# One layer of a hybrid attention decoder with experts, on one core: the loads of the first attention spread over three value tiles, the merge's reads group by group, and idle products moved and taken out

## The chip, the cores and the metric

The kernel runs on 1 core of one Trainium2 chip. The metric is the device time of one execution in microseconds (us); the times given are the median of 3 runs and their lowest and highest. All arithmetic is in float32.

## The reference, cut to what matters

The input x has 1024 tokens of 1024 channels. Per layer (there is one):

```
h = rmsnorm(x) * (1 + sc1) + sh1
proj = h @ w_in            # NSA q, keys/values, gates | dilated q/k/v | merge gates
o_nsa = g0 * compressed(q, kc, vc) + g1 * selected(q, ks, vs) + g2 * window(q, kw, vw)
o_dil = softmax-denominator mix of 3 dilated attentions (4 heads each)
merged = sigmoid(m0) * (o_nsa @ w_up_nsa) + sigmoid(m1) * (o_dil @ w_up_dil)
x = x + g1 * (merged @ w_o)
h = rmsnorm(x) * (1 + sc2) + sh2
x = x + g2 * experts(h)    # 32 experts, two per token, each silu(h@w1)*(h@w3) @ w2
out = rmsnorm(x)
```

"The first attention" is the native sparse attention (NSA): 8 heads in 4 pairs, each with a selected, a window and a compressed part. The second one is the dilated attention: 3 groups, each heads 0 to 3.

## The kernel before, in words

The program is a row of stages. At the end of a stage all engines meet, and no engine begins the next stage before the last one has arrived. The order on each engine (PE, DVE, ACT, POOL, and SP, which issues most transfers) is written out by hand, with semaphores between them. Transfers that SP issues go out in its program order.

**Condition and norm** (L242 to 485) makes h. It ends on PE with two idle products (L485). An idle product (L227) multiplies the identity by 512 columns of constants into a bank that nothing reads; it computes nothing that is used, and keeps PE at work.

**Projections** (L526 to 946). First come the rows of queries and keys, computed and stored to the DRAM tensor `d_qk`. Then come eight value tiles, v = 0 to 7. Each value tile is seven products (M1, M2, M6, M5, M7, M3, M4, in this order) that a Strassen-like scheme combines; DVE adds them up into four results (C11, C22, C12, C21). PE has four banks for them, so a product has to wait until DVE has used the product four before it (L890 to 892). For v of 4 and more every result goes into a staging slot of its own name (L603 to 607), and SP stores it to `d_v` (L645 to 649, and L622). DVE may fill the slot again in the next tile only when the store of the last one has landed (L813 to 814). At v = 4 (`HT`) SP also issues, behind the four stores of that tile, what the first attention needs (L650 to 661): 4 transfers of keys, 4 of queries (one for each pair of heads, L657) and, from `load_bias` (L969), 6 of bias. After the last tile PE has one idle product (L944).

**NSA** (L1011 to 1246) has 64 steps: for a pair of heads and a tile of 128 queries one step of selected scores, and one of window and compressed scores. In step s PE does the scores of step s, the transposes of step s - 1 and the value sums of step s - 2. It may not write the scores of step s before DVE has taken those of step s - 1 (`s_biased`, L1108 to 1110). In steps 0 and 1 there is little or nothing of the other two kinds of work.

**Dilated** (L1259 to 1468) has 6 sets in the order (i, g): sets 0 and 3 are group 0, sets 1 and 4 group 1, sets 2 and 5 group 2. SP stores each set to `d_dil`; sets 0 to 3 are waited for inside the stage (L1352), set 4 counts on `s_dil4`, and set 5 is stored by the first lines of the next stage and counts on `s_dil`. PE ends the stage with a wait for DVE's last bias and one idle product (L1408, L1409).

**Merge** (L1500 to 1835). SP issues the store of set 5, waits for sets 4 and 5 (L1546, L1547), and reads all three groups back into `dl` (L1548 to 1550). DVE, after its first additions, waits for all three (L1602), mixes the groups (`join_weights`, `join_group`) and makes `o_dil` (L1719). PE meanwhile does the products of channel tiles c = 0 and the first two of c = 1, and then turns `o_dil` (L1816), which waits for it.

**Out** (projection by w_o, router) and **experts** follow. The experts' weights are 32 x 6 MB; SP issues each 2 MB matrix when the slot that it goes to has come free, the last of them in a ring of ten slots.

Of the kernel before, what the change touches and what calls it, by code (L numbers as in the profile page):

```python
# [27 lines left out]
P = 128  # L28
# [6 lines left out]
NSA_H, NSA_KV = 8, 2  # L35
# [31 lines left out]
R_Q, R_CK, R_CV, R_SK, R_WK, R_DQ = 0, 512, 640, 768, 896, 1024  # L67
# [159 lines left out]
def idle_products(pe, k, bank, n):  # L227

    for _ in range(n):
        pe.matmul(k.psum[:, bank, :], k.ident, k.const[:, 0:BANK], start=True, stop=True)  # L230
# [11 lines left out]
def stage_condition_and_norm(k, hT, room, oT, hold, vD, ahead):  # L242

    nc = k.nc
    with ExitStack() as mem:
# [174 lines left out]
        @block.tensor  # L420
        def _(pe):
            pe.wait_ge(s_vec, 80)
            pe.wait_ge(s_const, 16)
            pe.transpose(k.psum[:, 0, 0:104], vec[:, :], k.ident[0:104, 0:104]).then_inc(s_vecps, 1)
            def turn(t):
                pe.wait_ge(s_xn, t + 1)
                for c in (2 * t, 2 * t + 1):
                    if c >= 4:
                        pe.wait_ge(s_evd if by_dve(c - 4) else s_eva, evacs[c - 4][0 if by_dve(c - 4) else 1])
                    for j in range(4):  # L430
                        d0 = (4 * (c % 2) + j) * P
                        tr = pe.transpose(k.psum[:, 4 + c % 4, j * P:(j + 1) * P], xs[:, t, d0:d0 + P], k.ident)
                    tr.then_inc(s_tr, 1)

            def bias():
                pe.wait_ge(s_oh, 32)
                pe.wait_ge(s_mask, 2)
                pe.wait_ge(s_vecT, 1)
                for i, cols in enumerate(bias_cols):
                    j, n = i % 4, cols.stop - cols.start  # L440
                    mm = pe.matmul(k.psum[G * j:G * (j + 1), B_BIAS[i // 4], 0:n], relb[:, :], onehot[:, cols],
                                   start=True, stop=True)
                    if j == 3 or i == nbias - 1:
                        mm.then_inc(s_bps, 1)

            def mod_row(i):
                if i in (1, 2):
                    pe.wait_ge(s_brow, i)
                if i == 3:
                    pe.wait_ge(s_row, 1)  # L450
                for kk in range(KD):
                    if kk == 0 or (i == 3 and kk == 4):
                        pe.wait_ge(s_ada[i + kk // 4], 16)
                    j = kk % 4
                    mm = pe.matmul(k.psum[G * j:G * (j + 1), B_ROW[i], :], condw[:, kk, :], ada(i, kk),
                                   start=(kk < 4), stop=(kk >= 4))
                mm.then_inc(s_rowps, 1)

            def mod_cols(i):
                pe.wait_ge(s_row, i + 1)  # L460
                if i == 0:
                    pe.wait_ge(s_brow, 4)
                if i == 2:
                    pe.wait_ge(s_row, 2)
                for j in range(4):
                    at = ADA_AT[i] // P + j
                    mm = pe.matmul(k.psum[:, B_COL[i // 2], at:at + 1], modrow[:, i % 2, j * P:(j + 1) * P],
                                   k.const[:, K_SEL:K_SEL + 1], start=True, stop=True)
                mm.then_inc(s_cols, 1)

            for t in range(NT):
                turn(t)
            bias()
            pe.wait_ge(s_wide, 1)
            mod_row(0)
            mod_row(1)
            mod_cols(0)
            mod_row(2)
            mod_cols(1)
            mod_row(3)  # L480
            mod_cols(2)
            mod_cols(3)
            pe.wait_ge(s_evd, evacs[-1][0])
            pe.wait_ge(s_eva, evacs[-1][1])
            idle_products(pe, k, 4, 2)  # L485


RUNS = (
# [37 lines left out]
def stage_projections(k, hT, vS, vD, gates, room, kc, vc, spare, ahead, g2row):  # L526
# [5 lines left out]
    with ExitStack() as mem:  # L532
# [55 lines left out]
        HT, HK = NT // 2, KD // 2  # L588
# [40 lines left out]
        @block.sync  # L629
        def _(sp):  # L630
            for g, (col, col2, row, scale) in enumerate(pairs):
                if g == 0:
                    continue
                if g >= 2:
                    sp.wait_ge(s_done, done(g - 2, M4))
                for s, c in enumerate((col, col2)):
                    sp.dma_start(wq[g % 2][s], w_in[:, :, c:c + P]).then_inc(s_w[g % 2], 16)
            sp.wait_ge(s_done, done(npairs - 1, M4))
            sp.wait_ge(s_used, used(npairs - 1, C21))
            for kv in range(2):  # L640
                sp.dma_start(w1c[:, kv], k.cmp_w1[0, kv].rearrange("(l p) n -> p l n", p=P)).then_inc(s_cw, 16)
                sp.dma_start(w2c[:, kv], k.cmp_w2[0, kv].rearrange("(c p) n -> p c n", p=P)).then_inc(s_cw, 16)
            for s in range(2):
                sp.wait_ge(s_store[s], 16 * npairs)
            for v in range(NV):  # L645
                for c in (C11, C22, C12, C21):
                    if set_of(v, c) > 0 and (v, c) != (NV - 1, C21):
                        sp.wait_ge(s_vused, vused(v, c))
                        store_values(sp, v, c)
                if v == HT:  # L650
                    sp.wait_ge(s_hid, 4)
                    for br, row in ((0, R_SK), (1, R_WK)):
                        for x in range(2):
                            sp.dma_start(ahead.keys[DH * x:DH * (x + 1), br, :, :],
                                         k.d_qk[row:row + P, :].rearrange("(h d) t -> d h t", d=DH)).then_inc(ahead.s_keys, 16)
                    for i in range(NSA_H // 2):
                        sp.dma_start(spare[:, i, :], k.d_qk[R_Q + P * i:R_Q + P * (i + 1), :]).then_inc(ahead.s_q[i], 16)  # L657
                    for c in (C21, C22):
                        sp.wait_ge(s_vst[SLOT[c]], 16 * stores_of(c, HT - 1))
                    sp.wait_ge(s_table, 1)  # L660
                    ahead.load_bias(sp, k, 0)
            sp.wait_ge(s_out, 3)

        @block.gpsimd
# [190 lines left out]
        def _(pe):  # L855
# [66 lines left out]
            for v in range(NV):  # L922
# [18 lines left out]
                    compressed_hidden()  # L941
                if v == HT:
                    compressed_out()
            idle_products(pe, k, 3, 1)  # L944

        return lambda sp: store_values(sp, NV - 1, C21)

# [63 lines left out]
def stage_nsa(k, vS, vD, gates, kc, vc, o_nsa, q, ahead, turned, store_last_values):  # L1011
# [5 lines left out]
    with ExitStack() as mem:  # L1017
# [27 lines left out]
        NS = len(steps)  # L1045
        OUT = 7
# [54 lines left out]
        def _(pe):  # L1101
            pe.wait_ge(s_keys, 64)
            for s in range(NS + 2):
                if s < NS:
                    i, t, kinds = steps[s]
                    if s % (2 * NT) == 0:
                        pe.wait_ge(s_q[i], 16)
                    for x in range(2):  # L1108
                        if s >= 1:
                            pe.wait_ge(s_biased, soft_no(s - 1, len(steps[s - 1][2]) - 1, x))  # L1110
                    for n, kind in enumerate(kinds):
                        lo, off = low(t, kind), offset(t, kind)
                        for col in range(0, width(t, kind), BANK):
                            for x in range(2):
                                half = slice(DH * x, DH * (x + 1))
                                w = min(BANK, width(t, kind) - col)
                                rhs = (kc[half, x, (i // 2) * NC:(i // 2 + 1) * NC] if kind == CMP else
                                       keys[half, kind - 1, i // 2, lo * P + col:lo * P + col + w])
                                at = (off + col) % BANK
                                mm = pe.matmul(k.psum[:, 2 * x + (off + col) // BANK, at:at + w],  # L1120
                                               q[half, i, t * P:(t + 1) * P], rhs, start=True, stop=True)
                                if col + BANK >= width(t, kind):
                                    mm.then_inc(s_scores, 1)
                v = s - 1
# [11 lines left out]
                v = s - 2  # L1136
                if 0 <= v < NS:
                    i, t, kinds = steps[v]
# [120 lines left out]
def stage_dilated(k, vD, spare, turned, hold, g2row, add_last):  # L1259
# [4 lines left out]
    with ExitStack() as mem:  # L1264
# [24 lines left out]
        NS = len(steps)  # L1289
# [74 lines left out]
        def _(pe):  # L1364
            for s in range(NS + 3):
# [14 lines left out]
                v = s - 2  # L1380
# [11 lines left out]
                v = s - 3  # L1392
                if 0 <= v < NS:
                    n, slot = steps[v]
                    i, g = sets[n]
# [9 lines left out]
                                               vD[:, g, slot + m + 1 - ntiles(v, m) + j, 2 * i + x, :],  # L1405
                                               start=(j == 0), stop=(j == ntiles(v, m) - 1))
                    mm.then_inc(s_summed, 1)
            pe.wait_ge(s_biased, 4 * NS)  # L1408
            idle_products(pe, k, 0, 1)  # L1409

        @block.scalar
        def _(act):
# [87 lines left out]
def stage_merge(k, hT, oT, o_nsa, room, mT, g1row, g2row, w_o, hold, s_wo, store_last_set):  # L1500
# [5 lines left out]
    with ExitStack() as mem:  # L1506
# [36 lines left out]
        @block.sync  # L1543
        def _(sp):
            store_last_set(sp)
            sp.wait_ge(k.s_dil4, 32)  # L1546
            sp.wait_ge(k.s_dil, 32)  # L1547
            for g in range(DIL_G):  # L1548
                sp.dma_start(dl[:, g].rearrange("p t h c -> p t (h c)"),
                             k.d_dil[g].rearrange("(t p) h c -> p t (h c)", p=P)).then_inc(s_dl, 16)  # L1550
            for row, c in ((g1row, 2 * D), (g2row, 5 * D)):
# [1492 lines left out]
```

## Time and profile before

| what | value |
|---|---|
| median of 3 runs | 1719.24 us (1719.05 to 1720.77) |
| the profiled execution's own time | 1718.73 us |
| its span, first to last instruction | 1716.9 us |
| PE busy | 1602.3 us (93%) |
| DVE busy | 673.9 us (39%) |
| ACT busy | 403.1 us (23%) |
| POOL busy | 176.2 us (10%) |
| mean granted TensorE clock | 0.982 of full |
| HBM read and written | 323.48 MB, 48.50 MB |

A granted clock of 1.00 is 2.4 GHz and 0.50 is 1.2 GHz. PE's busy time includes the time in which it works at the lower clock, and the idle products. In a line of a timeline the first number is the start, the second the time that the merged instructions take together, and the brackets hold the idle time of that engine just before, and who ended it. One float32 product of 128 x 128 by 512 columns shows as two MATMULs.

### The profile page before, as it was taken

Reading aid. Unit: us, or ns where it says so; the run is one execution under the profiler, and the core shown is the slowest. Engines: PE = TensorE matmul, PEld = TensorE weight load, DVE = VectorE, ACT = ScalarE, POOL = GpSimd, SP = SyncE. Lnnn points to the kernel's source line nnn. Section 1 sums busy time; section 2 is a strip of 40 time slices with the busy share of each in tenths; the row PEclk is TensorE's granted clock in tenths of the full one; section 3 lists DMA queues with packets and bytes.
Section 4 is the critical chain, followed back from the end, with each engine's and each line's share of the span. In section 5 each row is a group of like instructions: output and inputs, shape, how many; then the busy total and the mean of one; then the engine's idle time right before and its main releaser. Section 6 shows DMA issues by size and latency. Waiting matters only on the chain. (4 is left out here: it accounts for less than half of the span.)

```text
span 1716.9 us, 37104 instructions
## 1 busy us (share of the span) xinstructions
PE 1602.3 (93%) x15957; PEld 1039.2 (61%) x15957; DVE 673.9 (39%) x1682; ACT 403.1 (23%) x897; POOL 176.2 (10%) x220
## 2 busy tenths in 40 slices
PE   5999999998999999999999999999999999999873
PEld 3444445896777787644444445556777776676652
DVE  3533324312767667766654456562101001000003
ACT  4100000002666667510010002212121211211112
POOL 1205000000111010000000000001111111111100
PEclk8999999998999999999999999999999999999997
DMA  9874232235111007434352162289999999999996
GB/s 345 263 222 108 84 98 99 76 102 173 35 44 45 33 3 241 122 104 132 115 155 86 38 245 111 86 341 366 356 391 395 386 382 399 392 391 404 410 406 259
DMA packets 163745, 362.38 MB, mean 211 GB/s; under 512 B 28631, under 2 KB 111183, under 8 KB 138971
## 3 DMA queue, kind: packets, MB, share of 16 engines
q1 hardware_dynamic: 141456, 316.12, 50.1%
q0 software_dynamic: 12608, 28.01, 6.2%
q10 hardware_dynamic: 9516, 15.85, 2.6%
q8 instruction: 129, 2.11, 0.5%
q14 instruction: 36, 0.29, 0.1%
HBM read 323.48 MB, written 48.50 MB: 217 GB/s over the span
## 5 line engine op out<-in xcount | busy, mean ns | idle before, releaser
L2779 DVE TENSOR_TENSOR sb_m_hT<-psum,sb_m_sg 128x256 f32<-128x256 f32 (+2 forms) x32 | 15.3, 477 | 299.7 <-PE psum L2895 299.7
L2616 ACT ACTIVATE sb_w_o_sb<-psum,sb_rowmod 128x64 f32<-128x64 f32 (+2 forms) x256 | 81.7, 424 | 206.4 <-PE psum L2883 206.4
L862 PE MATMUL psum<-sb_vD,sb_room 128*128 128x512 f32 x240 | 104.7, 592 | 0.2 <-DVE sb_vD L743 0.2
L2895 PE MATMUL psum<-sb_w_o_sb,sb_front 128*64 128x64 f32 (+2 forms) x2560 | 91.0, 231 | 11.9 <-issue 7.3
L2895 PEld LDWEIGHTS psum<-sb_w_o_sb,sb_front 128*64 128x64 f32 x2560 | 89.0, 138 | 18.8 <-issue 18.2
L1179 ACT ACTIVATE sb_d_probs<-sb_d_probs,sb_d_nmax 128x640 f32<-128x640 f32 (+7 forms) x128 | 92.9, 735 | 12.6 <-DVE sb_d_nmax L1220 12.1
L1777 PE MATMUL psum<-sb_w_o_sb,sb_room 128*128 128x512 f32 x192 | 85.7, 603 | 0.0
L862 PEld LDWEIGHTS psum<-sb_vD,sb_room 128*128 128x128 f32 x240 | 45.5, 190 | 57.9 <-issue 57.9
L1148 PE MATMUL psum<-sb_vS,sb_room 128*64 128x65 f32 x2112 | 80.0, 226 | 0.3 <-ACT sb_room L1166 0.3
L1133 PE MATMUL psum<-sb_const,sb_d_probs 128*128 128x128 f32 x528 | 77.3, 283 | 1.6 <-ACT sb_front L1179 0.7
L1166 ACT COPY sb_room<-psum 128x512 f32<-128x512 f32 (+1 forms) x108 | 59.3, 549 | 82.6 <-PE psum L1133 82.6
L1120 PE MATMUL psum<-sb_front 64*128 64x512 f32 (+3 forms) x384 | 76.0, 500 | 2.9 <-DVE sb_d_nmax L1220 2.2
L1148 PEld LDWEIGHTS psum<-sb_vS,sb_room 128*64 128x64 f32 x2112 | 70.0, 138 | 11.3 <-issue 9.5
L753 DVE SCALAR_TENSOR_TENSOR sb_n_b_sel<-psum,sb_room 128x512 f32<-128x512 f32 x40 | 33.3, 832 | 105.5 <-PE psum L862 105.5
L1753 ACT ACTIVATE sb_room<-sb_room 128x2048 f32<-128x2048 f32 x8 | 15.3, 1910 | 246.4 <-DVE sb_room L1599 246.4
L862 PE MATMUL psum<-sb_rows,sb_room 128*128 128x512 f32 x160 | 71.1, 592 | 0.0
L1133 PEld LDWEIGHTS psum<-sb_const,sb_d_probs 128*128 128x128 f32 x528 | 58.4, 142 | 20.0 <-ACT sb_front L1179 7.3
L2627 ACT ACTIVATE sb_m_sg<-psum 128x256 f32<-128x256 f32 (+2 forms) x32 | 13.6, 425 | 238.4 <-PE psum L2895 238.4
L2895 PE MATMUL psum<-sb_w_o_sb,sb_mT 128*64 128x64 f32 (+2 forms) x1664 | 60.2, 231 | 7.7 <-issue 5.1
L2895 PEld LDWEIGHTS psum<-sb_w_o_sb,sb_mT 128*64 128x64 f32 x1664 | 58.2, 138 | 13.8 <-issue 13.8
L2895 PE MATMUL psum<-sb_w_o_sb,sb_room 128*64 128x64 f32 (+2 forms) x1536 | 59.5, 238 | 7.5 <-issue 6.0
L2895 PEld LDWEIGHTS psum<-sb_w_o_sb,sb_room 128*64 128x64 f32 x1536 | 57.9, 138 | 12.4 <-issue 12.1
(466 smaller groups left out, 2702.1 us busy)
## 6 DMA issues: line engine op xcount, KB each, us to landing
sb_front<-in_exp_w_dram SPq DMA_DIRECT2D x30, 2048.0 KB, 24.0
sb_mT<-in_exp_w_dram SPq DMA_DIRECT2D x20, 2048.0 KB, 26.6
sb_room<-in_exp_w_dram SPq DMA_DIRECT2D x18, 2048.0 KB, 23.9
sb_rows<-in_exp_w_dram SPq DMA_DIRECT2D x18, 2048.0 KB, 23.3
sb_w_o_sb<-in_exp_w_dram SPq DMA_DIRECT2D x10, 2048.0 KB, 25.1
sb_g_ada<-in_ada_w_dram SPq DMA_DIRECT2D x16, 1024.0 KB, 5.2
d_qk<-sb_n_b_sel ACTq DMA_DIRECT2D x20, 512.0 KB, 3.4
sb_front<-in_w_in_dram SPq DMA_DIRECT2D x16, 512.0 KB, 5.3
```

The source lines that it names most:

```text
L753: dve.scalar_tensor_tensor(dst, split(k.psum[:, bank(g, i), :]), scale, split(src), ALU.mult, ALU.add).then_inc(s_used, 1)
L862: mm = pe.matmul(k.psum[:, bank(g, i), :], w[:, kk, :], x[:, kk, :], start=(kk == 0), stop=(kk == KD // 2 - 1))
L1120: mm = pe.matmul(k.psum[:, 2 * x + (off + col) // BANK, at:at + w], q[half, i, t * P:(t + 1) * P], rhs, start=True, stop=True)
L1133: mm = pe.transpose(k.psum[:, 4 + c % 3, pos * P:(pos + 1) * P], tile(v, n, x)[:, j * P:(j + 1) * P], k.ident)
L1148: mm = pe.matmul(k.psum[DH * h:DH * (h + 1), OUT, col:col + DH + 1], turned[c % TURNED][:, pos * P + DH * h:pos * P + DH * (h + 1)], rhs, ...
L1166: act.copy(turned[c % TURNED][:, 0:n], k.psum[:, 4 + c % 3, 0:n]).then_inc(s_cact, 1)
L1179: act.activation(p, p, ACT.Exp, scale=-1.0, bias=nmax[:, no % 16:no % 16 + 1]).then_inc(s_probs, 1)
L1753: act.activation(sg[c % 2], sg[c % 2], ACT.Sigmoid).then_inc(s_sig, 1)
L1777: mm = pe.matmul(k.psum[:, bank(c, i), :], wt[:, kk, :], x[:, kk, :], start=(kk == 0), stop=(kk == HK - 1))
L2616: last = act.activation(dst[:, kk, 0:w], src, ACT.Identity, scale=k.rowmod[:, 0, kk:kk + 1], bias=k.rowmod[:, 1, kk:kk + 1])
L2779: tt(hT[:, :, 0:width[b]], hidden_ps(1, width[b]), sg[:, :, 0:width[b]], ALU.mult).then_inc(s_hid, 1)
L2895: mm = pe.matmul(k.psum[part, which, c * w:(c + 1) * w], view[:, kk, first:first + 2 * CAPS - 1:2], x[:, kk, 0:w], start=(kk == 0), stop=( ...
```

## The change

Four things are done. The loads for the first attention are split: the keys and the first pair's queries stay in value tile 4, the bias goes to value tile 5, and the other three pairs' queries go to value tile 6. The merge stage reads group 0 at once, group 1 when set 4 is stored, group 2 when set 5 is stored. In NSA, PE gets three idle products in step 1 and two in step 2, ahead of the wait for DVE. One of the two idle products of the first stage, that behind the value tiles, and that at the end of the dilated stage (with the wait ahead of it) are taken out.

```diff
@@ end of condition and norm, PE @@
-            idle_products(pe, k, 4, 2)
+            idle_products(pe, k, 4, 1)
@@ projections, SP @@
+            def load_queries(some):
+                for i in some:
+                    sp.dma_start(spare[:, i, :], k.d_qk[R_Q + P * i:R_Q + P * (i + 1), :]).then_inc(ahead.s_q[i], 16)
+
             for v in range(NV):
...
-                    for i in range(NSA_H // 2):
-                        sp.dma_start(spare[:, i, :], k.d_qk[R_Q + P * i:R_Q + P * (i + 1), :]).then_inc(ahead.s_q[i], 16)
+                    load_queries((0,))
+                if v == HT + 1:
                     for c in (C21, C22):
                         sp.wait_ge(s_vst[SLOT[c]], 16 * stores_of(c, HT - 1))
                     sp.wait_ge(s_table, 1)
                     ahead.load_bias(sp, k, 0)
+                if v == HT + 2:
+                    load_queries(range(1, NSA_H // 2))
@@ end of projections, PE @@
-            idle_products(pe, k, 3, 1)
@@ NSA, PE @@
                         pe.wait_ge(s_q[i], 16)
+                    if 1 <= s <= 2:
+                        idle_products(pe, k, OUT, 4 - s)
                     for x in range(2):
@@ end of dilated, PE @@
-            pe.wait_ge(s_biased, 4 * NS)
-            idle_products(pe, k, 0, 1)
@@ merge, SP @@
             store_last_set(sp)
-            sp.wait_ge(k.s_dil4, 32)
-            sp.wait_ge(k.s_dil, 32)
             for g in range(DIL_G):
+                if g >= 1:
+                    sp.wait_ge((k.s_dil4, k.s_dil)[g - 1], 32)
                 sp.dma_start(dl[:, g].rearrange("p t h c -> p t (h c)"),
```

## Rows read from the trace of the kernel before

**Rows 1.** Timeline of PE, value tiles 6 and 7.

```profile
387.47 1.89 PE L894 MATMUL psum<-sb_b_wvd,sb_vD 128*128 128x256 f32 x8
394.21 3.78 PE L894 MATMUL psum<-sb_b_wvy,sb_rows 128*128 128x256 f32 x8 [4.85 <-DVE sb_room L815]
...
400.03 3.62 PE L894 MATMUL psum<-sb_b_wvd,sb_rows 128*128 128x256 f32 x16
403.49 3.62 PE L894 MATMUL psum<-sb_n_b_sel,sb_vD 128*128 128x256 f32 x16
```

**Rows 2.** Timeline of DVE, value tile 6 and the end of tile 7.

```profile
393.73 0.42 DVE L815 TENSOR_TENSOR sb_room<-psum,sb_g2row 128x256 f32<-128x256 f32 x1 [12.49 <-DMA d_v<-sb_room]
...
412.38 0.42 DVE L815 TENSOR_TENSOR sb_room<-psum,sb_front 128x256 f32<-128x256 f32 x1 [1.36 <-PE psum L894]
```

**Rows 3.** Timeline of SP's issues in value tiles 4 to 7.

```profile
370.01 2.64 SPq L654 DMA_DIRECT2D sb_front<-d_qk  x4
372.69 2.02 SPq L657 DMA_DIRECT2D sb_front<-d_qk  x4
...
379.71 14.80 SPq L625 DMA_DIRECT2D d_v<-sb_room  x5
```

**Rows 4.** From issue to landing, the four query loads of L657.

```profile
DMA to landing us min/median/max: 12.2/13.2/14.4
```

**Rows 5.** Windows of 1 us; the last three columns: granted clock, DMA share, GB/s.

```profile
392.00:393.00 1.00, 0.00 (x0) 0.00 (x0) 0.00 (x0) 0.00 (x0) 0.00 (x0) 0.50 1.10 380
...
416.00:417.00 1.00, 0.59 (x2) 0.19 (x2) 0.87 (x8) 0.37 (x2) 0.00 (x0) 0.50 0.89 340
```

**Rows 6.** Timeline of PE, scores of NSA steps 0, 1, 2 and 5.

```profile
413.59 0.49 PE L1120 MATMUL psum<-sb_front 64*128 64x128 f32 x4 [0.45 <-PEq L532]
415.31 0.49 PE L1120 MATMUL psum<-sb_front 64*128 64x128 f32 x4 [1.23 <-DVE sb_d_nmax L1220]
...
417.21 1.22 PE L1120 MATMUL psum<-sb_front 64*128 64x256 f32 x4 [0.61 <-DVE sb_d_nmax L1220]
...
427.06 0.92 PE L1120 MATMUL psum<-sb_front 64*128 64x384 f32 x4
```

**Rows 7.** Timeline of PE, scores of NSA steps 34 and 37 (third pair, same shapes).

```profile
536.80 0.70 PE L1120 MATMUL psum<-sb_front 64*128 64x256 f32 x4 [0.15 <-DVE sb_d_nmax L1220]
...
543.49 0.92 PE L1120 MATMUL psum<-sb_front 64*128 64x384 f32 x4
```

**Rows 8.** Timeline around the end of the first stage.

```profile
46.59 2.26 DVE L417 TENSOR_SCALAR sb_rows<-sb_rows,sb_modA,sb_mod 128x1024 f32<-128x1024 f32 x3
...
49.16 7.10 PE L862 MATMUL psum<-sb_rows,sb_n_b_sel 128*128 128x512 f32 x16 [1.25 <-PEq L245]
```

**Rows 9.** Timeline of PE, end of dilated and first part of merge.

```profile
712.87 1.13 PE L230 MATMUL psum<-sb_const 128*128 128x512 f32 x2
714.29 3.68 PE L1768 MATMUL psum<-sb_const,sb_room 128*128 128x128 f32 x32 [0.30 <-PEq L1264]
...
741.85 7.03 PE L1777 MATMUL psum<-sb_rows,sb_front 128*128 128x512 f32 x16
751.70 1.94 PE L1768 MATMUL psum<-sb_const,sb_g_ada 128*128 128x128 f32 x16 [2.83 <-DVE sb_g_ada L1719]
```

**Rows 10.** Timeline of DVE in the same stretch.

```profile
712.97 0.43 DVE L1442 COPY sb_e_last_stage<-psum 128x260 f32<-128x260 f32 x1 [0.40 <-PE psum L1403]
...
725.76 0.68 DVE L1599 TENSOR_TENSOR sb_room<-psum,sb_room 128x512 f32<-128x512 f32 x1
731.12 0.22 DVE L1603 TENSOR_TENSOR sb_g_mn<-sb_mT 128x32 f32<-128x32 f32 x1 [4.67 <-DMA sb_mT<-d_dil]
```

**Rows 11.** Timeline of SP's issues in the same stretch.

```profile
714.24 0.92 SPq L1324 DMA_DIRECT2D d_dil<-sb_e_last_stage  x2
719.82 2.41 SPq L1549 DMA_DIRECT2D sb_mT<-d_dil  x3
```

**Rows 12.** Windows, part of the experts; columns as in rows 5.

```profile
1180.00:1300.00 120.00, 115.01 (x1923) 87.94 (x1921) 11.80 (x16) 19.00 (x55) 16.90 (x13) 1.00 1.00 377
```

## The prediction

> **What bounds the kernel now.** PE is busy for 93% of the span, so I read first the page's slices, where its granted clock drops, and then the places where PE sits idle. Four places belong to this change. (a) In value tile 6 PE stands 4.85 us between M7 and M3 [rows 1]; DVE, whose addition it waits for, stood 12.49 us itself, until a store of `d_v` had landed [rows 2]. That store was issued behind 14 loads [rows 3]. By the 1 us windows the clock is at 0.50 (1.2 GHz) at 392 us [rows 5], and the spacing of PE's products shows it full again (2.4 GHz) by 400 [rows 1]. (b) In the first NSA steps PE waits three times for a short while, 0.45, 1.23 and 0.61 us [rows 6], and in the 1 us windows the clock is at 0.50 at 416 [rows 5]; at 427.06 the scores of 384 columns take the 0.92 us that they take at full clock [rows 6, 7]. (c) At the boundaries ahead of NSA and of the merge, an idle product is what PE does last [rows 6, 9]. (d) In the merge DVE waits 4.67 us for the read of `d_dil` [rows 10], and PE, much later, 2.83 us for what DVE makes of it [rows 9]. After these places comes the stream of expert weights, with the DMA engines full [rows 12]. Its first transfers are released by PE and DVE in the stages before, so I expect an earlier merge to move all of it.
>
> **Part 1, loads over three tiles.** At full clock two products are spaced 403.49 - 400.03 = 3.46 us, one 1.73 us [rows 1]. M7 of tile 6 starts at 387.47, so M3 should start at 389.20 and tile 7 at 389.20 + 3.46 = 392.66. It starts at 400.03: **7.37 us lost**, 5.01 us of it idle (to 394.21) and 2.36 us because M3 and M4 ran mostly at half clock. What becomes of that? Now only keys and one pair of queries, 5 loads of 512 KB, are ahead of the first store of tile 5. The query loads, issued from 372.69 on, landed 12.2 us later at the soonest [rows 3, 4], thus the first of them at about 384.9; it was the fifth load. The store is issued behind it, so it lands at about 385 to 387 instead of 393.7. DVE wants to fill that slot when M2 of tile 6 is done, two products (M6, M5) before M7, at 387.47 - 3.46 = 384.0 [rows 1]; but PE is held only from 389.20 on. So DVE is late by up to 3 us and PE not at all, with 2 to 4 us to spare. Next in line: the bias (6 loads, 1.8 MB) is issued after tile 5's stores, about 381, and is down by about 390; the first store of tile 6 goes out behind it and has until about 401 minus the 7.4 us gained, 394. Then the three query loads, 1.5 MB, go out with tile 6's last store at about 393, and only the last tile's stores are behind them; nobody refills those slots. The bias is wanted at the first step of NSA, some 15 us after it lands, the other queries an attention pair later. SP's own order costs nothing: its issues are 0.5 us each. Taken: -7.4; bounds 0 (the store still lands too late) and -7.4.
>
> **Part 2, idle products in steps 1 and 2.** One idle product is two MATMULs of 512 columns. Eight products of that shape take 7.03 us [rows 9], so one costs 0.86 us once it is behind another. Before, scores of step 1 start 1.72 us after those of step 0, of step 2 1.90 us later [rows 6]. Now step 1 is behind some 0.35 us of scores and 3 x 0.86 = 2.58 us: 2.93, that is +1.2. Step 2 is behind about 1.1 us of scores and transposes and 1.72 us: 2.8, that is +0.9. **Cost +2.1 us**, since the products are longer than the waits that they fill. What they buy is the clock: from step 2 to step 5 it took 427.06 - 417.21 = 9.85 us, while the same shapes in the third pair, at full clock, took 543.49 - 536.80 = 6.69 us [rows 6, 7]: **-3.2**. Sum -1.1. Bounds: -3.2 (were the products hidden) and +4.3 (the clock falls all the same, and all five cost 0.86 us on top).
>
> The Trainium skill, page "TensorE: Matmul & The Clock Gate", section "Why this matters for your kernels", warns only of idle gaps of more than about 3 us between bursts. By that rule the waits here do no harm to the clock and the products only cost their 2.1 us; the total below would be -9.0 us. The trace speaks against it: the longest of the three waits was 1.23 us and the clock fell [rows 5, 6].
>
> **Part 3, idle product behind the value tiles.** PE ended at 413.59 - 0.45 = 413.14, DVE at 412.38 + 0.42 = 412.80 [rows 2, 6]. Without the product DVE is the last to arrive: **-0.3**.
>
> **Part 4, idle product at the end of dilated.** PE ended at 714.00 and the merge began at 714.29; DVE had ended at 713.40 [rows 9, 10]. Now about 713.7: **-0.6**. PE then idles some 0.8 us; the merge's own gap of 2.83 us left the clock full, since two more 512 column products, and turns, were around it [rows 9], so I put the clock at nothing here.
>
> **Part 5, reads by group.** The last two stores went out at 714.24, and the reads only at 719.82, when the stores had landed; they took until 731.12 [rows 10, 11], 11.3 us for 3.2 MB and the two bias rows behind them. Now group 0 goes out right behind the stores, at about 714.6, group 1 a little later, group 2 at about 719.2. Two thirds of the bytes then move while SP waits, and the last third, some 1.1 MB, lands by about 724. DVE asks for it at 726.44 [rows 10]: its wait of 4.67 us goes. DVE's chain from there to `o_dil` is its own work, with PE's products always done before it asks, so `o_dil` comes 4.67 us earlier, at 751.70 - 4.67 = 747.0. PE gets to the turn at 741.85 + 7.03 = 748.9 [rows 9]. So PE loses its 2.83 us wait, and DVE has 1.9 us to spare: **-2.8**, even if the reads land at 728. PE's next wait, 0.9 us for the copies of what was turned, stays. Bounds 0 and -2.8.
>
> **Part 6, first stage.** PE's idle time before the projections becomes 1.25 + 0.86 = 2.1 us. The stage does not end sooner, as DVE works until 46.59 + 2.26 = 48.85 [rows 8]. Cost 0 if the clock stays, by the nearest row, the 2.83 us gap that left it full [rows 9]; at most +2.4, what half clock cost after the long gap [rows 1]. I take 0.
>
> **Sum.** -7.4 - 1.1 - 0.3 - 0.6 - 2.8 = **-12.2 us**. The profiled execution took 1718.73 us, 0.5 below the median of the runs: 1706.5 against it, **1707.0** as a median.
>
> **The rivals.**
> 1. *The clock falls anyway in the first NSA steps.* For: the boundary gap ahead of the first scores grows from 0.45 to about 1.2 us, as the product there is gone, and scores and turns of 128 columns fill little. Against: the new products are dense work in the two later waits. Part 2 becomes +2.1 to +4.3 instead of -1.1; with +3.1 the time is 1711.2. Chance 0.13.
> 2. *The short waits are not what the clock fell by*, and the five products buy nothing: part 2 is +2.1, with what was lost at half clock lost as before, 1710.2. For it only that no single wait was long. Against: nothing else happened to PE before 416 [rows 5, 6]. Chance 0.03. This is the rule of "TensorE: Matmul & The Clock Gate" in the Trainium skill, weighed above.
> 3. *The clock falls in the first stage*, by the longer gap there: +2.4, 1709.4. Chance 0.12.
> 4. *Part of the stall in tile 6 stays*: the keys alone moved slowly, and their loads are still one block. If the store lands at 391, PE idles 1.8 us and pays the 2.4 us clock loss: 1711.2. For: the first queries landed 12.2 us after issue. Against: 2 to 4 us to spare. Chance 0.06.
> 5. *Saved time is lost in the expert stream*: 1719.2, no change. For: the DMA share there is 1.00 [rows 12]. Against: its start is released by the work before. Chance 0.03.
> 6. *Slower*: one block of loads that held up one store becomes three, and each holds up the store behind it as the old one did, in tiles 5, 6 and 7. At 7.4 us each that is 22.1 us instead of 7.4, the total -12.2 + 22.1 = +9.9: 1729. It turns slower from 4.1 us each on, that is 1.7 us idle and 2.4 us of clock. Against: each block is 1.5 to 2.6 MB instead of 6, and a result slot has a tile's 12 us to be stored. Chance 0.03.
>
> **How the numbers follow.** The forecast has 0.60. A change of 0.2% (3.4 us) is about what a measurement of this kernel can tell from none. Only rivals 5 and 6 are not faster by that: faster 0.94, within 0.03, slower 0.03. The range goes from 1704.0, by part 2's better bound (-3.2 instead of -1.1) and 0.9 us for the wait that I leave behind the turn, to 1712.5, which takes in rivals 1 to 4 and 1.3 us more. Rivals 5 and 6 lie outside, with what a wrong size in two parts at once would add.
>
> **What would show it.** Right: no idle time of PE before L894 over 1 us in tiles 6 and 7, and tile 7 beginning 12.1 us after tile 6; the first scores at about 405.9 on the new clock of the trace; scores of steps 0, 1, 2 spaced 2.9 and 2.8 us, and 6.7 us from step 2 to 5, with clock 1.00; DVE without a wait at L1603; the turn of L1768 with no wait for L1719; the expert stream the same from its first to its last transfer. Wrong: a granted clock of 0.50 just after the first scores or after 49 us; a DVE wait for a `d_v` store over 4 us; SP's first read of `d_dil` later than 716 less what was gained before.

## The result, and the profile after

The changed kernel takes **1708.63 us** (median of 6 runs, 1706.44 to 1710.9) against 1719.14 us before (6 runs, 1715.07 to 1720.77): ratio 0.9938, 95% interval 0.9924 to 0.9952, that is 10.5 us less. The forecast was 1707.0, 12.2 us less. The profiled execution took 1708.82 us with a span of 1707.0. The page of the changed kernel, its head and two rows of its slices:

```profile
span 1707.0 us, 37111 instructions
PE 1603.3 (94%) x15961; PEld 1038.2 (61%) x15961; DVE 675.0 (40%) x1682; ACT 404.0 (24%) x897; POOL 176.6 (10%) x220
...
PEclk9899999999999999999999999999999999999997
```

Line numbers from 641 on have grown by 4 to 7: L862 is now L868, L894 is L900, L1120 is L1127, L1768 is L1773. I compare the two traces by the time between landmarks on PE, so that a delay shows only where it arises. From first to last they are: the first projection product, value tile 5, the end of the value tiles, the scores of NSA steps 0, 2, 5 and 6, the merge's first product, its turn, the end.

| stretch on PE | before | after | difference | forecast |
|---|---|---|---|---|
| start to first projection product | 49.16 | 50.94 | +1.8 | 0 |
| to value tile 5 | 319.21 | 321.23 | +2.0 | 0 (part 6) |
| to the end of the value tiles | 43.91 | 36.52 | -7.4 | -7.4 (part 1) |
| to the first scores of NSA | 1.31 | 1.00 | -0.3 | -0.3 (part 3) |
| step 0 to step 2 | 3.62 | 5.87 | +2.2 | +2.1 (part 2) |
| step 2 to step 5 | 9.85 | 6.56 | -3.3 | -3.2 (part 2) |
| step 6 to the merge | 284.46 | 283.29 | -1.2 | -0.6 (part 4) |
| merge to its turn | 37.41 | 34.80 | -2.6 | -2.8 (part 5) |
| turn to the end | 965.20 | 964.02 | -1.2 | 0 |

Together that is the -9.9 us between the two profiled executions, 1718.73 and 1708.82.

The value tiles, PE's timeline of the changed kernel, tiles 6 and 7 (start, duration, engine, line, operation, tiles, form, count, and in brackets the idle time before and its releaser):

```profile
384.36 3.62 PE L900 MATMUL psum<-sb_b_wvd,sb_rows 128*128 128x256 f32 x16
387.81 3.62 PE L900 MATMUL psum<-sb_n_b_sel,sb_vD 128*128 128x256 f32 x16
391.26 1.89 PE L900 MATMUL psum<-sb_b_wvd,sb_vD 128*128 128x256 f32 x8
392.99 1.89 PE L900 MATMUL psum<-sb_b_wvy,sb_rows 128*128 128x256 f32 x8
394.72 1.89 PE L900 MATMUL psum<-sb_b_wvd,sb_front 128*128 128x256 f32 x8
396.44 3.62 PE L900 MATMUL psum<-sb_b_wvd,sb_rows 128*128 128x256 f32 x16
```

No idle time is left, tile 7 begins 12.08 us after tile 6, and every product takes what it takes at full clock. DVE, and SP's issues, in the same stretch:

```profile
388.90 0.42 DVE L821 TENSOR_TENSOR sb_room<-psum,sb_g2row 128x256 f32<-128x256 f32 x1 [3.87 <-DMA d_v<-sb_room]
```

```profile
376.48 0.61 SPq L647 DMA_DIRECT2D sb_front<-d_qk  x1
377.13 8.26 SPq L625 DMA_DIRECT2D d_v<-sb_room  x4
385.50 0.88 SPq L978 DMA_DIRECT2D sb_n_b_sel<-d_sel  x1
...
397.51 1.67 SPq L647 DMA_DIRECT2D sb_front<-d_qk  x3
```

DVE still waits for the store of tile 5, 3.87 us instead of 12.49 [rows 2]. PE's next product that has to wait for this addition, M3, begins at 391.26 + 1.73 = 392.99, and DVE was through at 388.90 + 0.42 = 389.32: 3.7 us to spare.

The first steps of NSA, PE's timeline of the changed kernel:

```profile
409.69 0.49 PE L1127 MATMUL psum<-sb_front 64*128 64x128 f32 x4 [0.99 <-PEq L532]
...
412.88 0.49 PE L1127 MATMUL psum<-sb_front 64*128 64x128 f32 x4
...
415.56 0.70 PE L1127 MATMUL psum<-sb_front 64*128 64x256 f32 x4
...
422.12 0.92 PE L1127 MATMUL psum<-sb_front 64*128 64x384 f32 x4
```

The scores of 256 columns take 0.70 us instead of 1.22 [rows 6]: full clock. The merge, PE, DVE and SP of the changed kernel:

```profile
708.18 3.68 PE L1773 MATMUL psum<-sb_const,sb_room 128*128 128x128 f32 x32 [0.79 <-PEq L1271]
742.98 1.94 PE L1773 MATMUL psum<-sb_const,sb_g_ada 128*128 128x128 f32 x16 [0.21 <-DVE sb_g_ada L1724]
```

```profile
722.39 0.22 DVE L1608 TENSOR_TENSOR sb_g_mn<-sb_mT 128x32 f32<-128x32 f32 x1 [2.06 <-DMA sb_mT<-d_dil]
```

```profile
708.14 0.94 SPq L1331 DMA_DIRECT2D d_dil<-sb_e_last_stage  x2
709.13 3.80 SPq L1554 DMA_DIRECT2D sb_mT<-d_dil  x3
```

PE's wait for what is turned fell from 2.83 to 0.21 us, and DVE's wait for the reads from 4.67 to 2.06 [rows 9, 10], where I had none left.

Last the first stage, where no gain and no loss was forecast. PE's timeline of the changed kernel, and windows of 5 us (busy time of each engine, then granted clock, DMA share, GB/s):

```profile
42.43 1.93 PE L455 MATMUL psum<-sb_vD,sb_a_condw 128*32 128x512 f32 x8 [1.92 <-DMA sb_vD<-in_ada_w_dram]
44.29 3.57 PE L467 MATMUL psum<-sb_const,sb_a_modrow 128*128 128x1 f32 x16
47.73 2.05 PE L230 MATMUL psum<-sb_const 128*128 128x512 f32 x2
50.94 9.55 PE L868 MATMUL psum<-sb_rows,sb_n_b_sel 128*128 128x512 f32 x16 [1.16 <-PEq L245]
```

```profile
45.00:50.00 5.00, 4.78 (x16) 3.20 (x16) 2.15 (x7) 1.24 (x1) 0.00 (x0) 0.50 0.00 0
50.00:55.00 5.00, 4.06 (x5) 1.85 (x6) 4.65 (x6) 0.00 (x0) 3.29 (x4) 0.50 0.61 165
55.00:60.00 5.00, 5.00 (x12) 2.15 (x11) 4.96 (x3) 0.60 (x1) 5.00 (x8) 0.91 1.09 359
```

The first two projection products take 9.55 us instead of 7.10 [rows 8], because they begin at half clock (0.50). Here the clock had fallen before the changed instruction was reached, when a part of `ada_w` came late: this one profile doesn't say whether the removed product is to blame.

### The profile page after: what moved, and what is told of

Same layout as the page of the kernel before. It is cut to its first block and busy times, and to the rows that moved or that the text cites. A ratio compares the mean times of both kernels' runs of the same rounds, so it can differ in the third digit from the quotient of the medians.

```text
span 1707.0 us, 37111 instructions
## 1 busy us (share of the span) xinstructions
PE 1603.3 (94%) x15961; PEld 1038.2 (61%) x15961; DVE 675.0 (40%) x1682; ACT 404.0 (24%) x897; POOL 176.6 (10%) x220
## 3 DMA queue, kind: packets, MB, share of 16 engines
q8 instruction: 129, 2.11, 0.5%
## 5 line engine op out<-in xcount | busy, mean ns | idle before, releaser
L868 PE MATMUL psum<-sb_vD,sb_room 128*128 128x512 f32 x240 | 104.6, 592 | 0.0
L868 PEld LDWEIGHTS psum<-sb_vD,sb_room 128*128 128x128 f32 x240 | 45.6, 190 | 57.4 <-issue 57.4
L1127 PE MATMUL psum<-sb_front 64*128 64x512 f32 (+3 forms) x384 | 74.2, 490 | 1.8 <-PEq L532 1.0
L868 PE MATMUL psum<-sb_rows,sb_room 128*128 128x512 f32 x160 | 71.1, 592 | 0.0
L2900 PEld LDWEIGHTS psum<-sb_w_o_sb,sb_mT 128*64 128x64 f32 x1664 | 59.1, 138 | 13.1 <-issue 12.6
```

The lines of the kernel that those rows point to most:

```text
L868: mm = pe.matmul(k.psum[:, bank(g, i), :], w[:, kk, :], x[:, kk, :], start=(kk == 0), stop=(kk == KD // 2 - 1))
L2900: mm = pe.matmul(k.psum[part, which, c * w:(c + 1) * w], view[:, kk, first:first + 2 * CAPS - 1:2], x[:, kk, 0:w], start=(kk == 0), stop=( ...
```

## The experiments

**My theory** after this reading: loads, reads and boundaries worked as forecast; the missing time lies in the first stage (rival 3) and in what the NSA products really give. The runs first take parts of the change alone, then undo parts. They come in three groups, and each group had its own runs of the kernel before: their median is 1718.46 us for e1 to e4, 1719.41 for e5 to e8 and 1719.43 for e9 to e12.

**e1, the split of the loads alone**, put into the kernel before:

```
...
+                    load_queries((0,))
+                if v == HT + 1:
...
+                if v == HT + 2:
+                    load_queries(range(1, NSA_H // 2))
```

> The kernel before with the split loads alone. Theory A (the parts add up as forecast): PE's 4.85 us wait in value tile 6 and the half clock behind it are gone, 7.4 us less than before, about 1711.8. Theory B (the missing 1.7 us of the forecast are in this part, as a store is still late): no more than 5.7 us less, and PE shows a wait of 1 us or more in tile 6 or 7. The first NSA steps stay at half clock in both, with 9.85 us from step 2 to step 5.

Measured: 1711.51 us, no idle time in the value tiles. The split alone is worth its 7 us, and nothing after it takes them back.

**e2, the reads by group alone**, put into the kernel before:

```
-            sp.wait_ge(k.s_dil4, 32)
-            sp.wait_ge(k.s_dil, 32)
             for g in range(DIL_G):
+                if g >= 1:
+                    sp.wait_ge((k.s_dil4, k.s_dil)[g - 1], 32)
```

> The kernel before with the reads by group alone. Theory A: 2.6 to 2.8 us less than before, about 1716.5, PE's 2.83 us wait for the turned sum down to 0.3 us or none, DVE's wait for the reads from 4.67 to about 2 us. Rival: the gain is taken back in the stages behind, less than 1 us in the total.

Measured: 1714.75 us, 3.7 below the kernel before; PE's part of it in the profile is 37.41 - 34.70 = 2.7. The tile 6 stall stays, with 4.86 us idle. The reads are worth their term in this kernel.

**e3, the changed kernel without the NSA products**:

```
-                    if 1 <= s <= 2:
-                        idle_products(pe, k, OUT, 4 - s)
```

> The changed kernel without the five idle products in NSA steps 1 and 2. Theory A: the clock falls after the first scores as it did before, step 2 to step 5 takes 9.8 us, steps 0 to 2 come 2.2 us sooner, total 1.1 us longer than the changed kernel. Rival C (short waits do not lower the clock): it stays full, and the kernel is 2.2 us faster than the changed one.

Measured: 1711.48 us, 2.9 above the changed kernel's 1708.63 and 2.5 above e4, so in the medians the products look worth more than forecast. But its profile has 11.36 us from step 0 to step 5, less than the 12.43 with the products: up to there they had cost 1.1 us against this draw. The profiled execution is the shortest of the twelve of e3 (1707.66 us), so it need not stand for the others.

**e4, the changed kernel with the three removed products back**:

```
-            idle_products(pe, k, 4, 1)
+            idle_products(pe, k, 4, 2)
...
+            idle_products(pe, k, 3, 1)
...
+            pe.wait_ge(s_biased, 4 * NS)
+            idle_products(pe, k, 0, 1)
```

> The changed kernel with the three idle products at stage ends put back (two in the first stage, one behind the value tiles, one at the end of dilated with its wait). Theory A: 0.9 us longer than the changed kernel, from the two later boundaries. Rival D (taking one out of the first stage costs clock, and that is the 1.7 us that the forecast missed): 0.5 to 1 us shorter than the changed kernel, with a full clock in the first value products.

Measured: 1709.0 us, 0.4 above the changed kernel, which is neither side's forecast. The profile shows both terms: 319.47 instead of about 321.1 us to tile 5, and +0.31 and +0.57 us at the two boundaries. Together that is 0.8 us less, and the medians don't show it.

**e5, the changed kernel again.**

> The changed kernel once more, as the measure for the three beside it: 1708.6 or so. Projections: from the first product to value tile 5, 320.5 to 321.3 us, as the clock is low in the first products.

Measured: 1708.93 us, 321.27 to tile 5, so the 2 us of the first stage came again; this time the clock was full ahead of the changed instruction and fell in the gap behind it.

**e6, two products in the first stage**, the rest as changed (first line of e4's diff):

> The changed kernel with two idle products at the end of the first stage again, nothing else. Theory D (the product taken out there cost clock): from the first product to value tile 5 it takes 319.2 to 319.5 us, and the total is 1 to 2 us shorter than the changed kernel. Theory A (it cost nothing, as forecast): no difference in either.

Measured: 1708.65 us, 319.39 to tile 5. The profile gives the 1.9 us back, the median 0.3 of it.

**e7, e6 with one and one product in the NSA steps** (`4 - s` becomes `1`):

> As the kernel with two in the first stage, but one idle product in NSA step 1 and one in step 2, instead of three and two: they fit into the waits, so steps 0 to 2 are spaced 1.73 and 1.9 to 2.0 us as without. Theory E (two suffice to hold the clock): steps 2 to 5 take 6.6 us and the kernel is 2 us faster than with three and two. Theory F (they do not): steps 2 to 5 take 7.7 to 9.9 us and the kernel is the same within 1 us.

Measured: 1706.73 us, 10.20 from step 0 to step 5. Up to step 5 one and one hold the clock and cost nothing in this profile; later PE has a wait that e8 doesn't have (see "The NSA products").

**e8, e6 with two and one** (`4 - s` becomes `3 - s`):

> The same with two products in step 1 and one in step 2: steps spaced 2.1 and 2.0 us. Theory E: steps 2 to 5 in 6.6 us, total 1.7 us faster than with three and two. Theory F: steps 2 to 5 in 7.7 us or more, total within 1 us of three and two.

Measured: 1705.03 us, 10.82 from step 0 to step 5, the lowest median so far; so it was run again.

**e9, the changed kernel a third time**, beside e10 to e12:

> The changed kernel once more, beside the three that follow. Its two profiles so far took 321.2 us from the first projection product to value tile 5, with the two products in front at half clock (9.55 and 9.60 us instead of 7.10), and 3.19, 2.68 and 6.56 us in the first NSA steps. Theory (the half clock in the first stage comes from the one product left there): again over 320.4 us and over 8.5 us, ratio about 0.994. Rival (chance of the draw): 319.2 us and 7.10 us this time.

Measured: 1708.02 us, 321.43 to tile 5, the theory's side for the third time.

**e10, e8 again.**

> Two idle products in the first stage, two and one in NSA steps 1 and 2, for a second time. Theory (the first stage gives 1.0 to 2.1 us, two products fewer in NSA 1.1 us, clock held all the same): 2 to 3.5 us below the changed kernel of this call, profile 319.2 us to value tile 5, 2.34, 1.92 and 6.56 us in the first NSA steps. Rival (the 3.9 us lead of its first run was the draw of the expert stream): within 1.5 us of the changed kernel.

Measured: 1705.03 us again, 3.0 below e9, and the forecast steps to 0.02 us. The theory holds.

**e11, e6 without NSA products:**

> Two idle products in the first stage, none in the NSA steps; everything else as changed. It differs from the kernel of three and two NSA products (1708.65 us) in these five alone. Theory (they cost 2.1 us and on average give back 1.8, at most 3.2): within 1 us of 1708.65, profile 1.73, 1.89 and 7.7 to 9.9 us from step 0 on. Rival a (they gain 1.1 us, as forecast): 1709.8. Rival b (by the draws of before taken with them, the stretch to the sixth step is always near 9.85): 1709.8 too, with 9.85 in the profile.

Measured: 1707.05 us, 1.6 below e6, which neither the theory nor the rivals had, with 9.46 us from step 2 to step 5. That is the long stretch of the kernel before once more. e6 is of another group; beside e10, of its own group, e11 is 2.0 us slower.

**e12, the changed kernel with the reads behind both waits** (e2's diff reversed):

> The changed kernel with the reads of the merge behind both waits again, as before. Theory (part 5 is worth 2.6 to 2.8 us on PE): 2.7 us slower than the changed kernel of this call, DVE waits about 4.7 us for the reads, PE waits about 2.8 us for what is turned, 37.4 us from the merge's first product to its turn instead of 34.8. Rival (the expert stream takes the time back): within 1 us of the changed kernel, with the 37.4 us in the profile.

Measured: 1707.38 us, 35.56 to the turn. Neither the theory nor the rival; see "The merge" below.

What was measured (us; the last four columns from each kernel's profile: first projection product to value tile 5; tile 5 to the end of the value tiles; NSA step 0 to step 5; merge to its turn):

| run | first stage, NSA products | median (range) | ratio, interval | to tile 5 | value | 0 to 5 | to turn |
|---|---|---|---|---|---|---|---|
| before | 2, none | 1719.14 | | 319.21 | 43.91 | 13.47 | 37.41 |
| after | 1, 3+2 | 1708.63 (1706.44-1710.9) | 0.9938 (0.9924-0.9952) | 321.23 | 36.52 | 12.43 | 34.80 |
| e1 | 2, none | 1711.51 (1707.25-1715.32) | 0.9961 (0.9947-0.9976) | 319.22 | 36.53 | 11.37 | 37.50 |
| e2 | 2, none | 1714.75 (1712.3-1719.37) | 0.9982 (0.9968-0.9996) | 319.21 | 44.56 | 12.35 | 34.70 |
| e3 | 1, none | 1711.48 (1707.66-1717.64) | 0.9954 (0.9937-0.9972) | 320.48 | 36.52 | 11.36 | 34.55 |
| e4 | 2, 3+2 | 1709.0 (1703.01-1711.28) | 0.9942 (0.9923-0.9962) | 319.47 | 36.53 | 12.43 | 34.51 |
| e5 | 1, 3+2 | 1708.93 (1706.7-1711.27) | 0.9942 (0.9919-0.9965) | 321.27 | 36.53 | 12.43 | 34.67 |
| e6 | 2, 3+2 | 1708.65 (1704.84-1709.78) | 0.9931 (0.9907-0.9954) | 319.39 | 36.53 | 12.43 | 35.23 |
| e7 | 2, 1+1 | 1706.73 (1703.94-1709.48) | 0.9924 (0.99-0.9949) | 319.22 | 36.52 | 10.20 | 34.63 |
| e8 | 2, 2+1 | 1705.03 (1703.12-1709.16) | 0.992 (0.9897-0.9944) | 319.22 | 36.52 | 10.82 | 35.09 |
| e9 | 1, 3+2 | 1708.02 (1706.36-1709.82) | 0.9938 (0.9922-0.9955) | 321.43 | 36.53 | 12.43 | 34.62 |
| e10 | 2, 2+1 | 1705.03 (1704.39-1707.0) | 0.9922 (0.9906-0.9938) | 319.21 | 36.53 | 10.82 | 35.04 |
| e11 | 2, none | 1707.05 (1702.36-1707.9) | 0.9928 (0.991-0.9945) | 319.22 | 36.52 | 13.53 | 34.54 |
| e12 | 1, 3+2 | 1707.38 (1706.06-1716.02) | 0.9943 (0.9923-0.9963) | 321.25 | 36.53 | 12.43 | 35.56 |

The intervals are 5 to 8 us wide, so these ratios can't settle a term of 1 or 2 us. The profiles' columns can, where kernels with the same instructions repeat to a tenth or two, as in the value tiles and with 3+2 products.

**The loads.** Every kernel with the split has 36.52 or 36.53 us and no idle time; both without it stall (43.91 and 44.56). That is 7.4 to 8.0 us, and e1's median lies 6.95 us below the kernel before. Nothing came back later.

**The first stage.** With two products, nine profiles took 319.21 to 319.47 us to tile 5, mean 319.26; with one, five took 320.48 to 321.43, mean 321.13. No value of the one group reaches the other: the removed product costs **1.9 us**. e5 shows how, with a full clock up to the product that was left. PE's timeline of e5, and windows of 1 us:

```profile
44.03 1.95 PE L467 MATMUL psum<-sb_const,sb_a_modrow 128*128 128x1 f32 x16
45.84 1.10 PE L230 MATMUL psum<-sb_const 128*128 128x512 f32 x2
49.05 9.60 PE L868 MATMUL psum<-sb_rows,sb_n_b_sel 128*128 128x512 f32 x16 [2.11 <-PEq L245]
```

```profile
46.00:47.00 1.00, 0.94 (x2) 0.11 (x1) 0.92 (x4) 1.00 (x2) 0.00 (x0) 1.00 0.00 0
47.00:48.00 1.00, 0.00 (x0) 0.00 (x0) 1.00 (x3) 1.00 (x2) 0.00 (x0) 0.62 0.00 0
48.00:49.00 1.00, 0.00 (x0) 0.00 (x0) 0.73 (x2) 0.60 (x1) 0.00 (x0) 0.50 0.00 0
54.00:55.00 1.00, 1.00 (x3) 0.38 (x2) 1.00 (x1) 0.00 (x0) 1.00 (x2) 0.96 1.22 267
```

The product ran at full clock, and the gap behind it was 2.11 us, just the 2.1 of the forecast. The clock fell in it, some 0.3 us after the product had ended, and stayed at 0.50 until 54. In e9 it fell 0.6 us into the same gap; in e3 it held through the gap and fell 0.1 us after the first projection product had begun. Where the clock had already fallen, as in the changed kernel's own profile, two products bring it back sooner; e10's timeline and window:

```profile
47.37 3.76 PE L230 MATMUL psum<-sb_const 128*128 128x512 f32 x4
51.43 7.11 PE L868 MATMUL psum<-sb_rows,sb_n_b_sel 128*128 128x512 f32 x16 [0.30 <-PEq L245]
```

```profile
51.00:52.00 1.00, 0.70 (x3) 0.36 (x3) 0.57 (x1) 0.00 (x0) 0.00 (x0) 0.81 0.00 0
52.00:53.00 1.00, 1.00 (x4) 0.51 (x3) 0.97 (x3) 0.00 (x0) 0.81 (x1) 1.00 0.43 84
```

The second product pays in both cases: with one, the half clock lasted 3.5 to 5.3 us into the projections, with two 1.4 us at most. Yet e6's median is only 0.3 us under e5's: 1.9 us is inside what those medians can't tell.

**The NSA products.** Without them the clock fell in all five profiles, 1.8 us (e11) to 3.9 us (e3) after the first scores, and for a time that varies. Steps 0 to 5 took 13.47, 11.37, 12.35, 11.36 and 13.53 us, mean 12.42; with 3+2 products always 12.43. In e1 and in e11, neither with products, windows of 1 us show the two ends of that spread:

```profile
409.00:410.00 1.00, 0.64 (x4) 0.34 (x4) 0.22 (x4) 0.98 (x4) 0.00 (x0) 0.80 1.00 350
410.00:411.00 1.00, 1.00 (x5) 0.68 (x4) 0.49 (x3) 0.00 (x0) 0.00 (x0) 0.50 0.88 285
...
413.00:414.00 1.00, 1.00 (x14) 0.75 (x12) 0.43 (x3) 0.03 (x1) 0.00 (x0) 0.99 1.15 275
```

```profile
410.00:411.00 1.00, 1.00 (x9) 0.88 (x9) 0.00 (x0) 0.24 (x1) 0.00 (x0) 0.50 0.87 315
...
420.00:421.00 1.00, 1.00 (x8) 0.64 (x6) 0.47 (x1) 0.06 (x1) 0.86 (x2) 0.92 0.86 191
```

About 3 us at half clock in e1 and 10 in e11; the kernel before had its 10 too (9.85 from step 2 to 5). So up to step 5, 3+2 products buy **0.0 us** on average over five profiles, against 1.0 by the one pair that I had. Two of the five, e1 and e3, are the shortest of their kernel's twelve runs, 4.3 and 3.8 us under its median, and they have the shortest half clock; a typical execution may lose more. Fewer products do better. e10's timeline:

```profile
408.16 0.49 PE L1127 MATMUL psum<-sb_front 64*128 64x128 f32 x4 [0.99 <-PEq L532]
408.58 1.98 PE L230 MATMUL psum<-sb_const 128*128 128x512 f32 x4
410.50 0.49 PE L1127 MATMUL psum<-sb_front 64*128 64x128 f32 x4
...
411.36 1.02 PE L230 MATMUL psum<-sb_const 128*128 128x512 f32 x2
412.42 0.70 PE L1127 MATMUL psum<-sb_front 64*128 64x256 f32 x4
```

With 2+1 the clock held in both profiles and steps 0 to 5 took 10.82 us, 1.6 less than with 3+2. With 1+1 (e7) it held in its one profile, and the products fit into the waits altogether: 1.72 us from step 0 to 1, as without any.

Step 5 is too early to stop counting, though. In the dilated stage all five kernels without NSA products have a wait of 0.3 to 1.5 us for the load of `sb_e_bias`; none of the eight with 3+2 or 2+1 has it, and e7, with 1+1, has it in full. PE's timeline of e7:

```profile
649.96 0.93 PE L1384 MATMUL psum<-sb_e_keys,sb_front 64*128 64x128 f32 x8 [1.24 <-DMA sb_e_bias<-d_dtab]
```

From the first scores to the merge's first product, less the 0.57 us of the product at the end of dilated where a kernel has it, the five kernels without NSA products took 298.75 to 300.13 us, mean 299.52; the six with 3+2 took 298.49 to 298.64, mean 298.52; e7 297.59; the two with 2+1 296.90 and 296.89. By the merge 3+2 are thus worth **1.0 us**, 2+1 2.6 and 1+1 1.9. Why the bias is waited for in some of these kernels and not in others stays open, so it isn't shown that the NSA products do that part.

**The merge.** Going back to the old reads gave PE a wait of 0.98 us, not 2.8. SP's issues of e12:

```profile
705.65 1.21 SPq L1328 DMA_DIRECT2D d_dil<-sb_e_stage  x2
707.92 0.94 SPq L1331 DMA_DIRECT2D d_dil<-sb_e_last_stage  x2
711.66 2.39 SPq L1554 DMA_DIRECT2D sb_mT<-d_dil  x3
```

The reads go out 3.74 us after the last stores, not 5.58 [rows 11], or 5.64 in e1: the stores were down sooner. Windows of 1 us behind them, first of the kernel before, then of e12:

```profile
716.00:717.00 1.00, 1.00 (x12) 1.00 (x10) 0.97 (x2) 1.00 (x4) 0.00 (x0) 1.00 0.92 274
717.00:718.00 1.00, 1.00 (x10) 1.00 (x9) 1.00 (x1) 1.00 (x4) 0.00 (x0) 1.00 0.10 19
718.00:719.00 1.00, 1.00 (x3) 0.39 (x3) 1.00 (x2) 0.97 (x2) 0.00 (x0) 1.00 0.08 17
```

```profile
710.00:711.00 1.00, 1.00 (x12) 1.00 (x10) 0.97 (x2) 1.00 (x3) 0.00 (x0) 1.00 0.71 213
711.00:712.00 1.00, 1.00 (x9) 0.76 (x7) 1.00 (x1) 1.00 (x4) 0.00 (x0) 1.00 0.00 0
```

Before, some bytes still move at 17 to 19 GB/s for 2 us ahead of the reads; in e12 none do. Part 4 is a suspect: without its product the last stores are issued 2.27 us behind the pair before them, with it 2.84. But e4, with the product and reads by group, issued its third read by 707.49 + 3.74 - 706.52 = 4.71 us after its last stores, as e9 did without it (4.70), while e2 took 5.60. So the spacing alone doesn't decide it, and the cause stays open. What is shown: the reads by group are worth 2.7 us where the stores land late (before against e2) and 0.3 to 1.0 where they land early (e12 against the kernels without the product, 34.54 to 35.23). The medians of e9 and e12 can't be told apart.

**A better version.** e10 (and e8) beats both kernels in the median: 1705.03 both times, 3.9 us below the changed kernel beside it (e5) and 3.0 (e9). From the profiles 1.9 + 1.6 = 3.5 was to be expected. The intervals against the kernel before still overlap for e9 and e10, but the runs themselves part: ten of the 12 runs of e8 and e10 lie below the lowest of the 12 of e5 and e9, 1706.36 us.

## Why the prediction was right, and where it wasn't

- **Part 1** (-7.4): shown, by after and e1. The store landed as worked out: M7 of tile 6 begins 3.79 us later than before [rows 1], so 388.90 is 385.1 on that trace's clock, and PE was not held. Rivals 4 and 6 are out: DVE waits behind one block, with 3.7 us to spare for PE. DVE's wait itself, 3.87 us, was just under the 4 us that were named as a sign of being wrong.
- **Part 2** (-1.1): both terms were right for the pair of profiles, +2.2 and -3.3. What was wrong is "from step 2 to step 5 it took 9.85 us", taken as *the* cost of the half clock: it was the long end of a spread from 7.74 to 9.85, and up to step 5 the part is worth 0.0 on average over five profiles. By the merge it is worth 1.0, near the forecast, but by way of a later wait that the forecast didn't have; that agreement is luck. Rival 1 did not come: with the products the clock was 1.00 in every profile. Rival 2, that short waits don't lower the clock, is out too; in e1 the clock fell behind waits of 0.45, 1.24 and 0.86 us (the windows above), which speaks against the rule that the prediction weighed. The same page of the Trainium skill, "TensorE: Matmul & The Clock Gate", section "A second HAM failure mode: psum-queue depth-cycling", does describe a clock that falls by frequent short idle times; these traces agree with that one.
- **Part 3** (-0.3): 1.00 us instead of 1.31 before the first scores in every kernel without the product; e4, with it, has 1.31.
- **Part 4** (-0.6): step 6 to the merge is 283.87 in e4 and 283.30 in e5 and e6, so -0.57. The rest of the -1.2 in the table is the wait for the load of `sb_e_bias` in dilated, 0.52 us before and none after. It is 1.0 to 1.5 us in e1, e2, e3 and e7, 0.3 in e11 and absent with 2+1 or 3+2 products. I didn't find its cause.
- **Part 5** (-2.8): the size is right, 2.6. Its landing time was not: I wrote that the last third of the reads is in by 724, and DVE waited until 722.39 + 6.11 = 728.5 on that clock (6.11 is how much sooner the merge began). The third read went out as forecast, at 712.56 + 6.11 = 718.7 against 719.2, but landed 9.8 us later, where I had left it 5. The forecast had said that 728 would do, and it nearly did: 0.21 us of PE's wait is left. What I took as fixed, and e12 shows isn't, is that the last stores are down 5.58 us after their issue. Where it is 3.74, the part is worth 1 us at most.
- **Part 6** (0) is the step that failed: "Cost 0 if the clock stays, by the nearest row, the 2.83 us gap that left it full." In e5 and e9 the gap came out as worked out, 2.11 us, but the clock fell in it; in e3 it fell just behind it, and in the other two profiles it was low already and came back later than with two products. Over the five that is +1.9 us on average, near the upper bound of 2.4. This was **rival 3**, with a chance of 0.12. The row chosen was near in length but not in what surrounds it. Ahead of the 2.83 us gap PE had run products of 512 columns for 30 us; here, in the last 3 us, it had run 8 products of one column and a single idle product. That this is the reason was not tested.
- **The expert stream** started earlier by what was saved and kept its length within its spread: 962.8 to 968.6 us from the turn to the end over all kernels. Rival 5 is out.

The account in medians: -12.2 forecast and +1.9 for part 6 gives -10.3, with part 2 at what it is worth by the merge; with part 2 at 0.0 it would be -9.2. Measured were -10.5, -10.5 and -11.4 against three sets of runs of the kernel before. The interval of the first ratio (8.3 to 13.1 us) holds both, so the medians don't decide on part 2. In the pair of profiles the miss of part 6 (+2.0) and the later start of the projections (+1.8) were made up in part by 0.6 us before the merge and 1.2 behind the turn, which no part of the forecast had: the nearness of the total owes something to luck.

## What to carry to other kernels

Price a half-clock stretch as a range even where a row shows it exactly, for here its length differed between runs of the same instructions; and before a gap is called harmless because another of its length was, look at what PE did ahead of both. Fill short waits sparingly: 2+1 products held the clock like 3+2 and cost 1.6 us less. Count a gain at a later landmark too: 1+1 were 0.6 us ahead of 2+1 at step 5 and 0.7 behind at the merge. Loads issued in one block here held up the store behind them; split by when each is wanted they cost nothing.

## What was not expected of the hardware

- In a gap of 2.11 us behind products of one column and one idle product the clock fell, 0.3 us after PE's last product (e5), while one of 2.83 us among products of 512 and 128 columns left it full [rows 9].
- With the same instructions and the same waits, the half clock lasted some 3 us in e1 and 10 us in e11.
- The reads that wait for the same two stores went out 5.58 us after the stores' issue in the kernel before and 3.74 in e12. The Trainium skill, page "Perfetto Trace Analysis", section "DMA Instruction — HWDGE (DVE, Sync)", says that a transfer's semaphore follows only when its write is confirmed, and that this can be surprisingly late for a write to HBM. The traces show the late semaphore, but in the kernel before also bytes that still move; the rule does not tell why these came late in one kernel and not in the other.
